# A decoder layer on one core: the first memory projections reordered, and other work moved around them

## The reference, cut to what matters

```python
h = rmsnorm(x, norm_mix_g)
qa, ka, va, cb, cc, cu, qx, glog = split(h @ w_in)
y_att  = moba_attention(qa, ka, va, rel_bias)          # logits + rel_table[t5_bucket(dist)]
y_conv = short_conv(cb, cc, cu, conv_w)
mem_n  = rmsnorm(mem, norm_mem_g)
kv     = mem_n @ w_mem_kv                              # 512 columns of keys, 512 of values
y_xatt = cross_attention(qx, kv)
merged = sum_i sigmoid(gates_i) * (y_i @ w_br_i)
x = x + merged @ w_out
x = x + moe_ffn(rmsnorm(x, norm_ffn_g))                # 32 experts, top 4, all experts' weights are read
return rmsnorm(x, norm_final_g)
```

## Time and profile before

| what | value |
|---|---|
| median of 3 runs | 1218.59 us (1218.15 to 1218.6) |
| the profiled execution, its own time | 1218.73 us |
| its span in the trace | 1216.9 us |
| PE busy | 1116.9 us, 92% |
| DVE busy | 385.0 us, 32% |
| ACT busy | 266.4 us, 22% |
| bytes moved by DMA | 452.09 MB, mean 372 GB/s |

### The profile page before, as it was taken

One profiled execution on the slowest core, in us unless ns is written; L12 is line 12 of the kernel. 1 busy time (PEld: TensorE's weight loads), 2 busy tenths in 40 slices (PEclk: granted clock), 3 DMA queues, 4 the chain that ended last, 5 costly groups with the idle time before them and its releaser, 6 DMA issues.

```text
span 1216.9 us, 15381 instructions
## 1 busy us (share of the span) xinstructions
PE 1116.9 (92%) x6085; PEld 582.1 (48%) x6085; DVE 385.0 (32%) x720; ACT 266.4 (22%) x406; POOL 4.6 (0%) x10
## 2 busy tenths in 40 slices
PE   7999999998999988888888888898898999988886
PEld 6999999985443333333333333333333333333332
DVE  6657654564231221212121212222222122121213
ACT  6334675433111111111111111111111111111112
POOL 0000000000000000000000000000000000000000
PEclk9999999999999999999999999999999999999998
DMA  8994444577999999999999999999999999999994
GB/s 271 351 293 139 138 156 168 214 284 310 427 425 425 427 427 426 426 427 425 427 425 428 425 428 425 427 425 425 425 426 426 428 427 426 427 427 426 424 426 179
DMA packets 74788, 452.09 MB, mean 372 GB/s; under 512 B 5074, under 2 KB 36167, under 8 KB 41991
## 3 DMA queue, kind: packets, MB, share of 16 engines
q1 hardware_dynamic: 73936, 449.79, 90.6%
q0 software_dynamic: 560, 1.74, 0.5%
q10 hardware_dynamic: 263, 0.15, 0.0%
HBM read 450.60 MB, written 1.06 MB: 371 GB/s over the span
## 4 chain that ended last, share of the span: by engine, by line
DMA 50%; PE 44%; DVE 4%; SPq 1%; issue 1%; ACT 1%; DVEq 0%; ACTq 0%
DMA dring<-in_w_down_dram 40%; PE bank L1034 19%; PE bank L1300 10%; DMA ring<-in_w_gu_dram 9%; PE bank L1336 9%; SPq L343 1%; DVE region_r L982 1%; DVE region_r L985 1%; DVE region_r L978 1%; PE bank L1320 1%; DVE region_r L979 1%; PE bank L1270 1%; PE bank L1221 1%; PE bank L1101 0%; PE bank L1081 0%
## 5 line engine op out<-in xcount | busy, mean ns | idle before, releaser
L1300 PE MATMUL bank<-ring,region_x 128*64 128x512 f32 x2048 | 449.6, 594 | 14.9 <-DMA ring<-in_w_gu_dram 14.9
L1336 PE MATMUL bank<-dring,region_r 128*64 128x512 f32 x1024 | 241.1, 607 | 55.3 <-DMA dring<-in_w_down_dram 54.3
L1300 PEld LDWEIGHTS bank<-ring,region_x 128*64 128x64 f32 x2048 | 143.0, 137 | 301.2 <-issue 273.4
L1336 PEld LDWEIGHTS bank<-dring,region_r 128*64 128x64 f32 x1024 | 68.0, 138 | 214.2 <-DMA dring<-in_w_down_dram 108.8
L978 DVE TENSOR_SCALAR region_r<-bank 128x512 f32<-128x512 f32 x32 | 22.1, 692 | 371.6 <-PE bank L1300 371.6
L996 DVE SCALAR_TENSOR_TENSOR y_parts<-bank,region_r,y_parts 64x512 fp32r<-64x512 f32 x32 | 23.8, 744 | 338.0 <-ACT y_parts L600 338.0
L591 ACT ACTIVATE region_r<-region_r 128x512 f32<-128x512 f32 x32 | 20.2, 632 | 436.6 <-DVE region_r L978 436.6
L1034 PE MATMUL bank<-hT_high,w_high 128*128 128x256 f32 x384 | 110.8, 289 | 0.0
L1034 PE MATMUL bank<-hT_low,w_high 128*128 128x256 f32 x384 | 108.6, 283 | 0.0
L1034 PE MATMUL bank<-hT_high,w_low 128*128 128x256 f32 x384 | 108.6, 283 | 0.0
L662 DVE TENSOR_TENSOR w_low<-ring,w_high 128x2048 fp32r<-128x2048 f32 x39 | 89.3, 2290 | 56.9 <-ACT w_high L448 56.8
(11 more groups left out here) (235 smaller groups left out, 909.2 us busy)
## 6 DMA issues: line engine op xcount, KB each, us to landing
ring<-in_w_gu_dram SPq DMA_DIRECT2D x128, 2048.0 KB, 29.7
dring<-in_w_down_dram SPq DMA_DIRECT2D x128, 1024.0 KB, 27.1
ring<-in_w_in_dram SPq DMA_DIRECT2D x26, 1024.0 KB, 10.8
ring<-in_w_mem_kv_dram SPq DMA_DIRECT2D x4, 1024.0 KB, 12.8
ring<-in_w_out_dram SPq DMA_DIRECT2D x4, 1024.0 KB, 4.8
ring<-in_w_br_conv_dram SPq DMA_DIRECT2D x2, 1024.0 KB, 7.0
ring<-in_w_br_att_dram SPq DMA_DIRECT2D x2, 1024.0 KB, 5.0
ring<-in_w_br_xatt_dram SPq DMA_DIRECT2D x2, 1024.0 KB, 5.4
```

Of the source, the lines that this page charges most:

```text
L1300: last = mm(ps[64 * half:64 * half + 64, :], xg[u // 2][:, c, 64 * (u % 2):64 * (u % 2) + 64], ring[:, slot0 + c, k * F + half * 512:k * F ...
L1336: last = mm(y_ps[64 * half:64 * half + 64, :], lhsT, dring[:, c // 2, at:at + 512], start=(c == 0), stop=(c == KC - 1))
```

## The change

- Memory values are projected before memory keys: `PROJ` takes j = 2, 3, 0, 1. The keys' row `rstd_row` is now copied inside DVE's `projection` of j = 0 (u = 2).
- SP loads the identity first (it was ACT's), then `mem` and piece 0 in alternating halves. Piece 1 goes ahead of `x`. ACT's queue begins with the rows.
- PE begins with 7 matmuls of ones whose result nobody reads, and puts 4 more behind each half of the `mem` transposes.
- The first projection is a function of its own, which goes through its parts as they become ready.
- The table's matmul moves behind the first projection, and the copy that raises `dist_sb` moves behind `w_low_part(2)` on DVE.
- The squares of `mem` move from ACT to DVE. On ACT `w_high_part(2)` moves ahead of `root(0)` and `root(1)`.

```diff
-PROJ = ([("w_mem_kv", 256 * j) for j in range(4)]
+PROJ = ([("w_mem_kv", 256 * j) for j in (2, 3, 0, 1)]
@@ SP
-        for t in range(TT):
+        sp.dma_start(consts[:, 0:P], a["consts"][:, 0:P]).then_inc(ident_in, 16)
+        first = ring[:, mixer_slot(0), :].rearrange("p (c n) -> p c n", c=KC)
+        first_src = a["w_mem_kv"][0, :, PROJ[0][1]:PROJ[0][1] + 256].rearrange("(c p) n -> p c n", p=P)
+        for t, landed in enumerate((first_half_in, piece_in[mixer_slot(0)])):
             sp.dma_start(mem_nat[:, t, :], a["mem"][0, t * P:(t + 1) * P, :]).then_inc(mem_in[t], 16)
-        p = 0
-        for name, col in PROJ:
-            if p == 1:
+            sp.dma_start(first[:, 4 * t:4 * t + 4, :], first_src[:, 4 * t:4 * t + 4, :]).then_inc(landed, 16)
+        p = 1
+        for name, col in PROJ[1:]:
+            if p == 2:
@@ ACT
-        act.dma_start(consts[:, 0:P], a["consts"][:, 0:P]).then_inc(ident_in, 16)
...
-        for u in range(4):
-            act_high_part(u, memT, memT_high)
-        act.wait_ge(piece_in[mixer_slot(0)], 16)
-        for half, ready in enumerate((w_high_half, w_high_ready)):
+        act_high_part(0, memT, memT_high)
+        act_high_part(1, memT, memT_high)
+        act.wait_ge(first_half_in, 16)
+        w_high_half_part(0, w_high_half)
+        act_high_part(2, memT, memT_high)
+        act.wait_ge(piece_in[mixer_slot(0)], 16)
+        w_high_half_part(1, w_high_ready)
+        act_high_part(3, memT, memT_high)
         w_high_part(1)
-        act.wait_ge(sq_done, TT)
         for t in range(TT):
             act.wait_ge(x_in[t], 16)
             square_sums(x_nat, squares, 1, t)
-        act.wait_ge(sq_done, 2 * TT)
+        act.wait_ge(sq_done, TT)
+        w_high_part(2)
+        root(0)
         root(1)
-        w_high_part(2)
@@ DVE
+        first_gain(0)
+        first_gain(1)
+        act_low_part(0, memT, memT_high, memT_low)
+        act_low_part(1, memT, memT_high, memT_low)
+        first_gain(2)
+        w_low_half_part(0, w_high_half, w_low_half)
+        first_gain(3)
+        w_low_half_part(1, w_high_ready, w_low_ready)
+        act_low_part(2, memT, memT_high, memT_low)
+        act_low_part(3, memT, memT_high, memT_low)
+        w_low_part(1)
+        for t in range(TT):
+            dve.wait_ge(mem_in[t], 16)
+            link(dve.scalar_tensor_tensor(region_r[:, 0:1024], mem_nat[:, t, :], 1.0, mem_nat[:, t, :], ALU.mult, ALU.mult,
+                                          accum_out=norm[:, 0, t:t + 1]))
+        rstd(0)
+        rstd(1)
+        dve.wait_ge(ident_in, 16)
+        for t in range(TT):
+            dve.tensor_scalar(rstd_diag[:, t, :], ident, norm[:, 0, 6 + t:7 + t], None, ALU.mult).then_inc(diag_ready, 1)
+        w_low_part(2)
         dve.wait_ge(dist_done, 1)
         dve.tensor_copy(bias_of_dist, bank[3][0:ATT_H, 0:TOEP]).then_inc(dist_sb, 1)
-        rstd(0)
...
-        w_low_part(1)
-        rstd(1)
-        w_low_part(2)
-        dve.wait_ge(rstd_row_done, 1)
-        dve.tensor_copy(rstd_row, bank[2][:, 0:256]).then_inc(rstd_row_sb, 1)
-        dve.wait_ge(rstd_row_sb, 1)
@@ DVE, projection
                 j = col // 256
+                if j == 0:
+                    dve.wait_ge(rstd_row_done, 1)
+                    dve.tensor_copy(rstd_row, bank[2][:, 0:256]).then_inc(rstd_row_sb, 1)
+                    dve.wait_ge(rstd_row_sb, 1)
@@ PE
+        pe.wait_ge(ones_ready, 1)
+        for _ in range(7):
+            mm(bank[3][:, 0:P], all_ones, all_ones, start=True, stop=True)
...
             transposed(mem_nat, u, bank[4 + u], hT_done)
-        pe.wait_ge(table_in, 16)
-        mm(bank[3][0:ATT_H, 0:TOEP], table, hot, start=True, stop=True).then_inc(dist_done, 1)
+            if u % 2:
+                for _ in range(4):
+                    mm(bank[3][:, 0:P], all_ones, all_ones, start=True, stop=True)
+
+        def first_projection():
+
+            high, low = [w.rearrange("p (c n) -> p c n", c=KC) for w in (w_high[0][:, :], w_low[mixer_slot(0)][:, :])]
+            for k in range(2):
+                dst, cut = bank[0][:, k * 256:k * 256 + 256], slice(k * P, k * P + P)
+                for half in range(2):
+                    cs = range(4 * half, 4 * half + 4)
+                    if k == 0:
+                        pe.wait_ge((w_high_half, w_high_ready)[half], 1)
+                    pe.wait_ge(act_high, 2 * k + half + 1)
+                    for c in cs:
+                        mm(dst, memT_high[:, c, cut], high[:, c, :], start=(c == 0), stop=False)
+                    pe.wait_ge(hT_parts, 2 * k + half + 1)
+                    for c in cs:
+                        mm(dst, memT_low[:, c, cut], high[:, c, :], start=False, stop=False)
+                    if k == 0:
+                        pe.wait_ge((w_low_half, w_low_ready)[half], 1)
+                    for c in cs:
+                        last = mm(dst, memT_high[:, c, cut], low[:, c, :], start=False, stop=(c == KC - 1))
+            last.then_inc(pieces_used, 1)
...
-        pe.wait_ge(hT_parts, 4)
+        first_projection()
+        pe.wait_ge(table_in, 16)
+        mm(bank[3][0:ATT_H, 0:TOEP], table, hot, start=True, stop=True).then_inc(dist_done, 1)
...
-            projection(p)
-            if p == 0:
-                pe.wait_ge(ones_ready, 1)
+            if p:
+                projection(p)
+            if p == 1:
                 pe.wait_ge(cols_sb, 1)
                 pe.wait_ge(diag_ready, TT)
```

More of the change, by code:

```diff
@@ L262, in build @@
     ident_in, consts_in = sem("ident_in"), sem("consts_in")
-    w_high_half, w_low_half = sem("w_high_half"), sem("w_low_half")
+    first_half_in, w_high_half, w_low_half = sem("first_half_in"), sem("w_high_half"), sem("w_low_half")
     ones_ready, diag_ready, rstd_row_done, rstd_row_sb = sem("ones_ready"), sem("diag_ready"), sem("rstd_row_done"), sem("rstd_row_sb")
@@ L455, in act_high_part, with w_high_half_part @@
             act.activation(dst[cut], src[cut], ACT.Copy).then_inc(act_high, 1)
-        for u in range(4):
-            act_high_part(u, memT, memT_high)
-        act.wait_ge(piece_in[mixer_slot(0)], 16)
-        for half, ready in enumerate((w_high_half, w_high_ready)):
+        def w_high_half_part(half, ready):
             cut = slice(half * 1024, half * 1024 + 1024)
             act.activation(w_high[0][:, cut], ring[:, mixer_slot(0), cut], ACT.Copy).then_inc(ready, 1)
[L463 to L466, removed]
+        act_high_part(0, memT, memT_high)
[6 more added lines that the diff above has]
+        act_high_part(3, memT, memT_high)
         w_high_part(1)
-        act.wait_ge(sq_done, TT)
         for t in range(TT):
@@ L570, in _ @@
             act.wait_ge(x2_sb, 2 * t + 2)
-            act.wait_ge(sq_done, 2 * TT + t)
+            act.wait_ge(sq_done, TT + t)
             square_sums(x2, squares2, 2, t)
@@ L630, in rstd @@
         def rstd(n):
-            dve.wait_ge(sq_done, TT * (n + 1))
+            if n:
+                dve.wait_ge(sq_done, TT * n)
             dve.tensor_scalar(norm[:, n, 2:4], norm[:, n, 0:2], 1.0 / D, EPS, ALU.mult, ALU.add).then_inc(mean_done, 1)
@@ L663, in w_low_part, with first_gain, w_low_half_part @@
                 .then_inc(w_low_ready, 1)
-        dve.wait_ge(cols_sb, 1)
-        for u in range(4):
+        def first_gain(u):
             dve.wait_ge(hT_done, u + 1)
             with_gain(bank[4 + u], g_mem, memT, u % 2, u // 2, gained)
[L669 to L672, removed]
+        def w_low_half_part(half, high, low):
             cut = slice(half * 1024, half * 1024 + 1024)
@@ L676, in _ @@
                               ALU.subtract).then_inc(low, 1)
-        dve.wait_ge(dist_done, 1)
-        dve.tensor_copy(bias_of_dist, bank[3][0:ATT_H, 0:TOEP]).then_inc(dist_sb, 1)
+        dve.wait_ge(cols_sb, 1)
+        first_gain(0)
[13 more added lines that the diff above has]
+                                          accum_out=norm[:, 0, t:t + 1]))
         rstd(0)
+        rstd(1)
         dve.wait_ge(ident_in, 16)
@@ L682, in _ @@
             dve.tensor_scalar(rstd_diag[:, t, :], ident, norm[:, 0, 6 + t:7 + t], None, ALU.mult).then_inc(diag_ready, 1)
-        w_low_part(1)
-        rstd(1)
         w_low_part(2)
-        dve.wait_ge(rstd_row_done, 1)
-        dve.tensor_copy(rstd_row, bank[2][:, 0:256]).then_inc(rstd_row_sb, 1)
-        dve.wait_ge(rstd_row_sb, 1)
+        dve.wait_ge(dist_done, 1)
+        dve.tensor_copy(bias_of_dist, bank[3][0:ATT_H, 0:TOEP]).then_inc(dist_sb, 1)
         def projection(u):
@@ L1004, in _ @@
         for t in range(TT):
-            dve.wait_ge(sq_done, 3 * TT + t + 1)
+            dve.wait_ge(sq_done, 2 * TT + t + 1)
             at = norm[:, 3, 4 + t:5 + t]
@@ L1024, in parts @@
             return [w.rearrange("p (c n) -> p c n", c=chunks) for w in (w_high[p % 3][:, :], w_low[mixer_slot(p)][:, :])]
-        def halves_of_first(chunks):
-            pe.wait_ge(w_low_half, 1)
```

(5 more changed lines are left out.)

## The result

The changed kernel takes 1223.52 us (median of 5 runs, 1222.09 to 1224.82), where the kernel before took 1218.59 (5 runs, 1217.84 to 1218.99). The ratio is 1.0041, with a 95% interval of 1.003 to 1.0051: about 4.9 us slower. The profiled execution took 1223.27 us, with a span of 1221.5, which is 4.6 over that of before.

A forecast was written before the change was run, and what follows sets the result against it. The experts' stream fills the DMA engines, so its start, set by PE's mixer program, fixes the end. On 1218.73 us, 5.0 late bias and 1.5 clock gave 1225.2, as a median 1225.1; range 1220.6 to 1228.5.

The forecast's parts named there:

- The clock: PE after standing 8 us ahead of the bias: may restart at the low level, costing 1.5 us (0 to 1.7).
- piece 2 lands: Load ahead of ACT's `w_high_part(2)`: lands at 18.8 us, give or take 0.5, with the same bytes ahead of it.
- `dist_sb` rises: DVE's copy of the table's product, behind `w_low_part(2)`: done at 25.3 us instead of 15.69, 9.65 later.
- write to DRAM: POOL's write of the table's product: 4.0 us instead of 5.2, bounds 3.0 and 5.2.
- read from DRAM: POOL's read of the bias back from DRAM: 6.3 us, as in the kernel before.
- SP goes on: SP's queue after its wait for the bias: issues piece 4 near 36.3 us, where it was 27.80.
- row copied, turning of the bias starts: PE's turning of the bias, behind DVE's copy of `rstd_row`: starts at 46.0 us, against 41.01 before.
- late bias: Mixer: the late chain through DRAM starts PE's turning of the bias 5.0 us later than before.
- The front: Start of the kernel: first projection ends between 16.8 and 19.3, winning 2 to 4.5 us, waited away behind the bias.
- start of projection 2: PE's projection 2, behind DVE's scaling of the values: starts at 26.2 us against 29.41 before, 3.2 us sooner.
- The rival that was faster: PE does not wait for the bias chain; the front's 3.2 us stay, giving 1215.4 us; chance 0.10.

The follow-up runs named there:

- e1: Changed kernel with the table's product back ahead of the first projection, its copy ahead of `w_low_part(1)`, squares of `mem` in another tile: 1215.86 us, ratio 0.9975.
- e2: Kernel before with one edit, DVE's copy of the table's product moved behind `w_low_part(2)`: 1220.68 us, ratio 1.002.
- e3: Changed kernel with 24 matmuls of ones keeping PE busy ahead of its wait for the bias: 1221.98 us, ratio 1.003.
- e4: Changed kernel, but SP issues piece 4 without waiting for the bias: 1220.68 us, ratio 1.0017.
- e8: Changed kernel without the 15 matmuls of ones: 1223.59 us, ratio 1.0041.
- e6: As e5, with DVE's copy of the row ahead of `w_low_part(4)`: 1213.64 us, ratio 0.9961 to the kernel before.
- e9: As e6, without the 15 matmuls of ones: 1215.94 us, ratio 0.9982 to the kernel before.
- e7: As e1, without the 15 matmuls of ones: 1216.04 us, ratio 0.998 to the kernel before.
- e5: As e1, with ACT's two roots ahead of `w_high_part(2)`: 1215.63 us, ratio 0.9975 to the kernel before.

## Why the prediction was right, point by point

The forecast was 1225.1 and the measured time is 1223.52, slower as forecast. The path is the one that the prediction followed: e1 takes the late copy out and the loss goes, e2 puts it alone into the old kernel and a loss comes. The clock is shown as a cost of its own by e3. The terms of the sum:

| step | predicted | measured |
|---|---|---|
| piece 2 lands | 18.8 | 19.8 |
| `dist_sb` rises | 25.3 | 25.75 |
| write to DRAM | 4.0 (3.0 to 5.2) | 1.9 |
| read from DRAM | 6.3 | 5.9 |
| SP goes on | 36.3 | 34.17 |
| row copied, turning of the bias starts | 46.0 | 44.18 |
| late bias, the turning against before | 5.0 | 3.0 |
| clock | 1.5 (0 to 1.7) | 2.3 to 2.5 |
| sum | 6.5 | 5.5 |
| time against before | 6.5 | 4.9 |

That the total is so close is in part luck. The late bias was put 2.0 us too high and the clock about 1.0 too low, and these errors offset each other. What the profile was to show is met in kind and smaller in size: SP's wait on the bias is longer by 6.3 us instead of 8, PE's idle time is 5.82 instead of 8, and the experts' stream starts 5.7 us later instead of 6.5.

- **Piece 2** came 1 us later. The prediction held the landing fixed because the bytes ahead of it are the same. The order of the queue isn't: SP issues it at 8.5, 3.8 us later than before, behind more and shorter transfers. That this is the reason is argued, not shown.
- **The write** is the term that I mis-sized most, outside my own bounds. I took a later small load of POOL's (3.8) for the nearest row. Of the 5.2 us of before, 3.3 were waiting beside the stream of pieces: the same 12 KB take 1.9 us with the queues empty (1.84 in e2, where nothing but the copy moved), and 5.3 in e4 with them full again. The Trainium skill's page "DMA: Bandwidth & Descriptors" (section "Anatomy of one DMA — SWDGE (gpsimd) path") gives about 2.0 us as the fixed part of such a transfer. The trace agrees with that for an empty queue. The estimate of 4.4 us by the fit on that page of the Trainium skill for the read of 1 MB isn't met: 5.9 alone, 9.9 beside the stream.
- **The clock** was priced from a stretch of matmuls that was at the low level for only its first part. The turning is made of two long matmuls, which the trace counts as four, and both fell into the slow time: 3.75 against 1.72, and another 0.5 in projection 4. The Trainium skill's page "TensorE: Matmul & The Clock Gate" (section "Why this matters for your kernels") has the rule that an idle gap between bursts of matmuls sends the engine back to its lower clock. The runs agree, with 0.50 granted behind 5.82 us.
- **The front** went better than predicted, with the first projection over at 16.4 instead of 16.8 to 19.3. It didn't matter, as predicted: PE reaches the turning 2.8 us sooner than before (38.36 against 41.17) and stands there until 44.18. e8 takes 1.6 us of the front away and the time stays. The start of projection 2, 26.59 against a predicted 26.2, was held by DVE's scaling of the values behind the copy.
- **The rival that was faster** needed `dist_sb` by 20.3. e1 has it near 14 and is faster, by 2.6 us where the rival gave 3.2.

**From 5.5 to 4.9.** SP's first load for the experts starts at 227.11 in the changed kernel (L347) and 221.59 in the one before (L343). Behind its last long rest, the stream goes on at 303.25 and 297.56. That is 5.5 and 5.7 us later, and PE's last run of L1379 (L1336 before) starts 5.6 us later. So the mixer's loss comes through the experts one for one, but the spans differ by only 4.6. The 1.1 us between are in what follows that run, by the chains of the kernel before and of the changed one:

```profile
1195.50 7.09 PE bank L1336 x32
1202.59 4.22 PE bank L1344 x8
1206.81 1.17 PE bank L1221 x2
```

```profile
1201.13 7.09 PE bank L1379 x32
1208.22 3.63 PE bank L1387 x8
1211.85 0.68 PE bank L1264 x2
```

The closing matmuls, the last two rows of each, take 5.4 us before and 4.3 in the changed kernel. In the kernel before the granted clock falls to 0.69 there, with PE busy all the time; in the changed kernel it stays at 1.00. The profiles show no link with the edits: the same work takes 4.3 us in e1, e4 and e6, 4.5 to 4.7 in e3, e8 and e9, 5.4 in e2 and e7, and 5.6 in e5. It also explains e6, whose last run of L1379 starts 4.1 us sooner than that of before and whose span is 5.2 us shorter. A difference of about 1 us between two versions is therefore better read from the start of the turning than from the time.

**What stays open.** I didn't find why the clock falls at the end in some executions and not in others, nor why piece 2 lands between 19.4 and 20.7 from one execution to the next. And I made no run of the changed kernel with the row alone copied early. In it the bias is in at 34.15, PE comes at 38.36, and what it waits for until 44.18 is DVE's copy of the row, behind the low part of piece 4. How much of the 5.82 us would go that way isn't known: projection 4 would still wait for that low part, until about 43.5.

## What to carry to other kernels

An instruction of half a microsecond can stand at the head of a chain of 19 us: before one moves it back in its engine's order, one follows what it raises through every queue, here a round trip through DRAM, a load that waits for it, two engines and a copy. A gain at the front counts only if nothing behind waits longer than it, so look at the wait that ends last further on, and time warm-up matmuls in an order that has no such wait. And when an engine waits for one late thing, look which innocent neighbour stands behind it in the order: here the copy of a row behind `w_low_part(4)` made PE wait where it hadn't to.

## What the runs showed of the hardware

- POOL's write of 12 KB to DRAM: 1.9 us with idle queues, 5.2 to 6.0 us beside streaming loads (before, e1, e4, e7). Its read of 1 MB: 5.9 to 6.3 us with the pieces held back (changed kernel, before) and 9.9 us beside the stream (e4).
- PE's granted clock fell to 0.50 around an idle time of 5.82 us (changed kernel) and around one of 3.19 us (e4, where the turning took 3.78 us); behind idle times of 1.63 us (e2) and 1.11 us (e1) it stayed at 1.00. It also fell with PE busy all the time, in the last matmuls of some executions (0.69 over 4 us in the kernel before, 1.00 in the changed one).
- Behind the 7 matmuls of ones, the first eight transposes ran at the high level in three executions (1.09 or 1.10 us in the changed kernel, e1 and e5), and in three others they didn't, or not from the start (1.65 us in e6, 1.97 in e3 and e4). Without the ones eight took 1.97 us (e7), and sixteen took 3.67 us in the kernel before.
- These levels are told by the length of the rows. The column of the granted clock stands at 1.00 from the start of the span, also where the kernel before spaces its matmuls by 0.21 us instead of 0.12.
